# Latent attention by heads: q's mean and root, the place of k, values of two pairs at once, and the output by tiles

## What is computed

```python
cq, ckv, k_rope = split(h @ w_dqkv, [384, 640])              # latents: 384, 256, 32
q  = (rms_norm(cq) @ w_uq).reshape(.., 16 heads, 96)         # 64 plain + 32 turned
kv = (rms_norm(ckv) @ w_ukv).reshape(.., 16 heads, 128)      # 64 of k, 64 of v
q_nope, k_nope = rms_norm(q_nope), rms_norm(k_nope)          # by head
q_rope, k_rope = apply_rope(rms_norm(q_rope)), apply_rope(rms_norm(k_rope))
s = (q_nope . k_nope + q_rope . k_rope) * 96 ** -0.5         # causal
o = softmax(s) @ v;   x = x + o @ w_o
```

## Time and profile before

| | us |
|---|---|
| median of three runs | 2913.57 |
| the runs | 2916.39, 2913.57, 2913.35 |
| the profiled execution, its own time | 2916.41 |
| its span | 2914.6 |
| PE busy in the span | 2871.7 |
| DVE, ACT, POOL busy | 1300.5, 567.2, 1849.9 |
| mean granted clock of PE, share of full speed | 0.994 |

### The profile page before, as it was taken

How to read it: one execution, slowest core, us unless ns; L and a number is a source line. 1 busy time by engine, 2 the same in 40 slices (tenths; PEclk the granted TensorE clock), 3 DMA queues, 4 the chain that set the end, 5 groups by cost and what they waited for, 6 DMA issues and landing times.

```text
span 2914.6 us, 36291 instructions
## 1 busy us (share of the span) xinstructions
PE 2871.7 (99%) x13536; PEld 2327.8 (80%) x13536; DVE 1300.5 (45%) x1506; ACT 567.2 (19%) x822; POOL 1849.9 (63%) x1822
## 2 busy tenths in 40 slices
PE   9999999999989999999999999999999999999998
PEld 6778887888867778888888888788888777788887
DVE  5765544414456655414444223443244555443241
ACT  4550221000124441000111101210001445300000
POOL 5557548777752228777785565677777444577775
PEclk9999999999999999999999999999999999999999
DMA  4112212232220002222232222222322111222322
GB/s 147 64 58 87 74 57 101 88 107 101 79 89 28 33 34 87 92 103 100 80 124 82 78 94 80 73 101 79 113 85 91 69 65 50 72 88 87 106 92 88
DMA packets 38582, 242.34 MB, mean 83 GB/s; under 512 B 4288, under 2 KB 4672, under 8 KB 16608
## 3 DMA queue, kind: packets, MB, share of 16 engines
q1 hardware_dynamic: 37296, 237.19, 23.4%
q10 hardware_dynamic: 1200, 3.96, 0.4%
HBM read 239.04 MB, written 2.10 MB: 83 GB/s over the span
## 4 chain that ended last, share of the span: by engine, by line
PE 92%; DVE 3%; POOL 1%; ACT 1%; DVEq 1%; issue 1%; ACTq 0%; DMA 0%; POOLq 0%; SPq 0%
PE ps L400 66%; PE ps L433 12%; PE ps L1344 1%; PE ps L1159 1%; PE ps L1300 1%; PE ps L1381 1%; POOL w_lo L702 1%; PE ps L1178 1%; PE ps L1361 1%; PE ps L1376 1%; PE ps L1394 1%; PE ps L1290 1%; POOL w_hi L714 1%; DVEq L2257 0%; DVEq L1852 0%
## 5 line engine op out<-in xcount | busy, mean ns | idle before, releaser
L714 POOL CAST w_hi<-raw 128x512 fp32r<-128x512 f32 (+1 forms) x909 | 677.4, 761 | 1047.3 <-PE ps L400 838.1
L702 POOL TENSOR_TENSOR w_lo<-raw,w_hi 128x512 fp32r<-128x512 f32 (+1 forms) x909 | 1222.0, 1356 | 0.1
L400 PE MATMUL ps<-h_hi,w_hi 128*128 128x512 f32 x1904 | 751.9, 395 | 3.3 <-DVE h_lo L1863 3.0
L400 PE MATMUL ps<-h_hi,w_lo 128*128 128x512 f32 x1904 | 742.0, 390 | 0.0
L400 PE MATMUL ps<-h_lo,w_hi 128*128 128x512 f32 x1904 | 741.5, 389 | 0.0
L400 PEld LDWEIGHTS ps<-h_hi,w_hi 128*128 128x128 f32 x1904 | 357.7, 188 | 80.7 <-issue 5.0
L400 PEld LDWEIGHTS ps<-h_lo,w_hi 128*128 128x128 f32 x1904 | 357.9, 188 | 75.8 <-issue 3.1
L400 PEld LDWEIGHTS ps<-h_hi,w_lo 128*128 128x128 f32 x1904 | 357.6, 188 | 75.2
L400 PE MATMUL ps<-a_hi,w_hi 128*128 128x512 f32 x816 | 320.1, 392 | 2.2 <-issue 1.4
L400 PE MATMUL ps<-a_lo,w_hi 128*128 128x512 f32 x816 | 318.4, 390 | 0.0
L400 PE MATMUL ps<-a_hi,w_lo 128*128 128x512 f32 x816 | 318.3, 390 | 0.0
(11 more groups left out here) (320 smaller groups left out, 3623.5 us busy)
## 6 DMA issues: line engine op xcount, KB each, us to landing
raw<-weights SPq DMA_DIRECT2D x169, 1024.0 KB, 4.9
raw<-weights SPq DMA_DIRECT2D x64, 704.0 KB, 4.1
raw<-weights SPq DMA_DIRECT2D x8, 640.0 KB, 3.9
raw<-weights SPq DMA_DIRECT2D x8, 512.0 KB, 3.6
x<-x_in SPq DMA_DIRECT2D x8, 256.0 KB, 6.9
x_out<-x SPq DMA_DIRECT2D x1, 2048.0 KB, 6.3
scr<-phase_ret ACTq DMA_DIRECT2D x1, 1536.0 KB, 8.0
scr<-phase_mla ACTq DMA_DIRECT2D x1, 640.0 KB, 6.7
```

Source lines behind the costliest of these rows:

```text
L400: mm = pe.matmul(out_ap, a, b, start=(i == 0 and not begun), stop=(i == n - 1 and ended))
L702: pool.tensor_tensor(w_lo[:, slot, parts[j]], raw[:, slot, parts[j]], w_hi[:, slot, parts[j]].bitcast(F32), ALU.subtract).then_inc(s_split ...
L714: pool.tensor_copy(w_hi[:, slot, piece], raw[:, slot, piece]).then_inc(s_hi[j], 1)
```

## The change

1. **q by heads.** The mean of q's squares of head 0 moves ahead of the turned scores of head 0 on PE. ACT takes the root of each head by itself, and DVE norms and turns each head by itself (512 columns an instruction instead of 1024).
2. **k earlier.** The product for k stands between the two turned scores. Where the pair has no v of its own to make, this product is the last reader of its chunk and gives the slot back.
3. **v of two pairs.** Even pairs' chunks hold v of two pairs (1536 columns), odd pairs' chunks none (1024). The product for v has 24 matmuls of 256 columns for two pairs, in two halves of 12, in banks 7 and 6. It is made in odd pairs, before the k mean and between the two products with the weights; for pairs 0 and 1 it is made ahead of the loop. ACT copies it out in four pieces.
4. **Head of the stage.** PE takes the first q mean when the kv root is there. DVE norms kv latent 0 before the second low part of q's squares, writes one copy of the turned k, and leaves the constants; ACT writes the constants and the second copy of the turned k.
5. **The output** is stored by eight DMAs, each when its tile of x is updated.

The diff, cut to what the prediction speaks of:

```diff
...
-STAGE_WIDTHS = {"ssd": [384] + [2048] * 15, "gla": [2048] * 15, "mla": [2048] * 3 + [1280] * 8 + [2048] * 4,
+STAGE_WIDTHS = {"ssd": [384] + [2048] * 15, "gla": [2048] * 15, "mla": [2048] * 3 + [1536, 1024] * 4 + [2048] * 4,
...
-            sp.wait_ge(s_res, 8 * n_res + 2)
-            sp.dma_start(out, x[:, :, :]).then_inc(s_out, 16)
-            sp.wait_ge(s_out, 16)
+            for k in range(KD):
+                sp.wait_ge(s_res, 8 * (n_res - 1) + k + 3)
+                sp.dma_start(out[:, k, :], x[:, k, :]).then_inc(s_out, 16)
+            sp.wait_ge(s_out, 16 * KD)
...
-                def kv_weights(par, k, at):
-                    at += 768 + 256 * k
-                    return [b[:, (c0 + 3 + par) % 2, at:at + P] for b in (w_hi, w_lo)]
+                def kv_weights(par, k, at, n):
+                    at += 768 + (P if par else 3 * P) * k
+                    return [b[:, (c0 + 3 + par) % 2, at:at + n] for b in (w_hi, w_lo)]
 
                 def proj_k(w, par):
                     pe.wait_ge(s_mln, 2 * w + 1)
-                    product(pe, ps[:, 6, :], [(*kv_weights(par, k, 0), h_hi[:, k, :], h_lo[:, k, :])
-                                              for k in range(2)]).then_inc(s_mpk, 1)
-
-                def proj_v(w, par):
-                    pe.wait_ge(s_mln, 2 * w + 2)
-                    for tb in range(TB):
+                    product(pe, ps[:, 6, :], [(*kv_weights(par, k, 0, P), h_hi[:, k, :], h_lo[:, k, :])
+                                              for k in range(2)]).then_inc(s_used if par else s_mpk, 1)
...
+                def proj_v(w, part):
+                    if part == 0:
+                        pe.wait_ge(s_mln, 2 * w + 2)
+                    else:
+                        pe.wait_ge(s_mr, 3 * w + 3)
+                    for tb in (2 * part, 2 * part + 1):
                         s = slice(tb * P, (tb + 1) * P)
-                        mm = product(pe, ps[:, 7, s], [(h_hi[:, k, s], h_lo[:, k, s], *kv_weights(par, k, P))
-                                                       for k in range(2)])
-                    mm.then_inc(s_used, 1)
...
-                def q_means(w):
-                    for e in range(2):
-                        pe.wait_ge(s_msl, 2 * w + e + 1)
-                        pe.matmul(ps[:, 6 + e, :], m_blkq, m_sqh[:, e, :], start=True, stop=False)
-                        pe.matmul(ps[:, 6 + e, :], m_blkq, m_sql[:, e, :], start=False, stop=True).then_inc(s_mm, 1)
+                        mm = product(pe, ps[:, 7 - part, (tb % 2) * 256:(tb % 2) * 256 + 256],
+                                     [(h_hi[:, k, s], h_lo[:, k, s], *kv_weights(0, k, P, 2 * P)) for k in range(2)])
+                    mm.then_inc(s_used if part else s_mvp, 1)
+
+                def q_mean(w, e):
+                    pe.wait_ge(s_msl, 2 * w + e + 1)
+                    pe.matmul(ps[:, 6 + e, :], m_blkq, m_sqh[:, e, :], start=True, stop=False)
+                    pe.matmul(ps[:, 6 + e, :], m_blkq, m_sql[:, e, :], start=False, stop=True).then_inc(s_mm, 1)
...
@@ -1206,19 +1211,24 @@
                         residual_begun("mla", (0, 1))
                     max_turned(u, 0)
                     max_turned(u, 1)
-                    if not ahead:
+                    if ahead:
+                        q_mean(u + 1, 0)
+                    else:
                         residual_begun("mla", (2,))
                     scores_turned(u, par, 0)
                     if ahead:
-                        q_means(u + 1)
+                        q_mean(u + 1, 1)
+                        proj_k(u + 1, nxt)
                     else:
                         residual_begun("mla", (3,))
                     scores_turned(u, par, 1)
                     if ahead:
-                        proj_k(u + 1, nxt)
-                        proj_v(u + 1, nxt)
+                        if par:
+                            proj_v(u + 1, 0)
                         k_mean(u + 1)
                     weighted(u, par, 0)
+                    if ahead and par:
+                        proj_v(u + 1, 1)
                     weighted(u, par, 1)
...
                 proj_q(0, 0, 0)
                 latent_sum(0, (3, 4))
                 proj_q(0, 0, 1)
-                q_means(0)
+                pe.wait_ge(s_mcr, 3)
+                q_mean(0, 0)
+                q_mean(0, 1)
                 pe.wait_ge(s_mh, 5)
                 proj_k(0, 0)
                 k_mean(0)
                 proj_v(0, 0)
+                proj_v(0, 1)
+                pe.wait_ge(s_mkrope, 2)
                 pair(0, 0, True, True)
...
+                act.activation(m_ident, phase_const("mla", "mla_ident"), ACT.Copy)
+                act.activation(m_mask, phase_const("mla", "mla_mask"), ACT.Copy)
+                act.activation(m_blkq, const("blkq"), ACT.Copy)
+                for e in range(2):
+                    act.activation(h_hi[:, 6 + e, :], x[:, e, :], ACT.Copy, scale=0.0)
...
-                def q_rstd(w):
-                    for e in range(2):
-                        act.wait_ge(s_mm, 3 * w + e + 1)
-                        act.activation(m_r[:, e, :], ps[:, 6 + e, :], ACT.Ln, bias=EPS).then_inc(s_mln, 1)
-                    settled().activation(m_r[:, 0:2, :], m_r[:, 0:2, :], ACT.Exp, scale=-0.5).then_inc(s_mr, 1)
-
-                def k_squared(w):
-                    act.wait_ge(s_mpk, w + 1)
+                def q_rstd(w, e):
+                    act.wait_ge(s_mm, 3 * w + e + 1)
+                    act.activation(m_r[:, e, :], ps[:, 6 + e, :], ACT.Ln, bias=EPS).then_inc(s_mln, 1)
+                    settled().activation(m_r[:, e, :], m_r[:, e, :], ACT.Exp, scale=-0.5).then_inc(s_mr, 1)
+
+                def k_squared(w, odd, n):
+                    if odd:
+                        wait_used(c0 + 3 + w)
+                    else:
+                        act.wait_ge(s_mpk, n + 1)
...
-                def pair(u, par, first, ahead):
+                def pair(u, par, ahead, n):
                     if ahead:
                         q_squared(u + 1)
+                        q_rstd(u + 1, 0)
                     exps(u, 0)
                     if ahead:
-                        q_rstd(u + 1)
+                        q_rstd(u + 1, 1)
+                        k_squared(u + 1, not par, n)
                     exps(u, 1)
                     if ahead:
-                        k_squared(u + 1)
-                        v_copied(u + 1, 1 - par, first)
                         k_rstd(u + 1)
+                    if ahead and par:
+                        v_copied(u + 1, n, 0, 0)
                     sums_inverted(u, 0)
+                    if ahead and par:
+                        v_copied(u + 1, n, 0, 1)
                     sums_inverted(u, 1)
-
+                    if ahead and par:
+                        for part in range(2):
+                            v_copied(u + 2, n, 1, part)
+
+                q_squared(0, True, (0,))
                 latent_rstd(3, m_csq[3], 0)
-                q_squared(0, True)
-                q_rstd(0)
-                k_squared(0)
+                q_squared(0, True, (1,))
+                q_rstd(0, 0)
+                q_rstd(0, 1)
+                k_squared(0, False, 0)
                 k_rstd(0)
-                v_copied(0, 0, True)
-                pair(0, 0, True, True)
+                act.wait_ge(s_mkrope, 1)
+                act.activation(m_k[64:112, 1, :, :], m_k[64:112, 0, :, :], ACT.Copy).then_inc(s_mkrope, 1)
+                for slot in range(2):
+                    for part in range(2):
+                        v_copied(0, 0, slot, part)
+                pair(0, 0, True, None)
...
                     dve.tensor_tensor(m_k[64:112, w, :, :], over_heads(m_kx[64:112, :]), over_heads(m_t[64:112, 0, :]),
-                                      ALU.add)
-
-                for w in range(2):
-                    rope_in_k(w)
+                                      ALU.add).then_inc(s_mkrope, 1)
+
+                rope_in_k(0)
...
-                def q_normed(w):
+                def q_ready(w, par, e):
                     dve.drain()
-                    dve.wait_ge(s_mr, 2 * w + 1)
...
+                    dve.wait_ge(s_mr, 3 * w + e + 1)
+                    dve.scalar_tensor_tensor(m_raw[:, e, :], m_raw[:, e, :], m_qgain, m_r[:, e, :], ALU.mult, ALU.mult)
                     dve.drain()
-                    turned_products(m_t, m_raw[:, 0:2, :], True)
-
-                def q_ready(par):
-                    dve.tensor_tensor(m_q[:, par, :, :], m_raw[:, 0:2, :], over_heads(cos), ALU.mult)
-                    settled().tensor_tensor(m_q[64:112, par, :, :], m_q[64:112, par, :, :], m_t[64:112, :, :], ALU.add)
+                    turned_products(m_t[:, e, :], m_raw[:, e, :])
+                    dve.tensor_tensor(m_q[:, par, e, :], m_raw[:, e, :], cos, ALU.mult)
```

(21 more changed lines are left out.)

44 lines of the change are left out of this document (24 added, 20 removed).

## The result

The changed kernel takes 2900.22 us (median of 4, 2898.72 to 2901.02), the kernel before in the same session 2914.82 (median of 4, 2913.35 to 2916.39): a ratio of 0.995, 95% interval 0.9938 to 0.9962. It is 14.6 us faster. The prediction was 2894 with a range of 2887 to 2900: the sign was right, the gain was forecast a third too large, and the time lies just above the range. The two profiled executions stand at 2916.41 and 2900.19 us, 16.2 apart where the sum said 20.0.

A forecast was written before the change was run, and what follows sets the result against it. TensorE (PE), busy 99% of the span, was taken as the bound. Terms -3.6 - 7.1 - 2.6 - 2.4 + 2.8 - 7.1 = -20.0 us gave 2893.6 on the median of 2913.57, stated as 2894, range 2887 to 2900.

The forecast's parts named there:

- DVE's new wait: Loop, scores after pairs 0, 2, 4, 6: PE waits 0.7 us for DVE's k each time, +2.8 us (0 to 8.4).
- S + 21.4: Even pairs: k ready 21.4 us after S, the start of a pair's scores, before POOL's cost of 2.3 us.
- S + 23.0: Even pairs: PE reaches the next scores 23.0 us after S, the start of a pair's scores.
- a rival of 3%: Scores after pairs 0, 2, 4, 6: waits grow to 3 us and the clock falls, +27 us, 2921; 3%.
- q's order by heads: Turned scores, seven pairs: head 0's mean fills PE's wait of about 0.34 us for DVE, -2.4 us.
- V of two pairs: Loop, pairs 2 to 7: 24 matmuls of 256 columns take 2.88 us for two pairs, not 5.26; -7.1 us.
- the -2.6 in pair 0: First pair's body: loses its whole V, since pair 1's V is made ahead of the loop; -2.6 us.
- The head: Start of the latent attention stage: -7.1 us, 5.2 from the earlier start and 1.9 from the scores' clock.
- Store by tiles: Kernel's end: seven of eight 256 KB stores land under PE's matmuls, the last takes 2.7 us; -3.6 us (-1.8 to -4).
- The fit that the prediction quotes for it: Output store: about 2.0 us plus bytes at 436 GB/s, 2.6 us for 256 KB, making the term -3.7.
- the clock comes back late: Stage's head: clock back only at 881.9, scores mostly at 1.2 GHz, -4.3 instead of -7.1, 2896 us; 22%.
- POOL blocks DVE outright: Even pairs: POOL's 4.2 us wholly in DVE's way, wait 2.1 in pairs 0, 2, 4, 6, +5.6, 2899 us; 15%.

## Why the prediction was wrong, step by step

- **The step that failed: DVE's new wait, +2.8 us forecast, 7.7 measured, and 1.7 more of clock.** Its mechanism was the right one, and its price too: POOL beside DVE was put at 2.3 us and measured at 2.35. Three inputs were off. k without POOL was ready at S + 21.55, 21.95, 21.70 and 21.70, not S + 21.4 (1.3 us over the four pairs). PE arrived at S + 22.73, not S + 23.0 (the terms written there give 23.08), since the steps by heads saved more than the shown wait (0.3, four times, 1.1). And "both casts and both subtractions of the 1024-wide chunk" was taken for all four even pairs, though behind pair 6 comes the output product's chunk of 2048 columns: 3.51 us instead of some 1.4, 2.1 more, and then the clock. 2.8 + 1.3 + 1.1 + 2.1 = 7.3, near the 7.7. The order of the chunks was in the code, and nothing of pair 6 had to be guessed.
- **The clock after a wait.** The forecast had it as a rival of 3% that needs 3 us in all even pairs. It came in one pair, at 3.5 us. With q's roots together it came in all four, at 4.3 each; its total of +27 us was met there by parts that were each off, which is luck.
- **q's order by heads: -2.4 forecast.** B of the kernels without V of two pairs gives -5.0 in six pairs, so about -5.8 in seven. The waits view shows 0.34 us per pair. In the pair of the earlier trace rows another 0.07 us of idle time lies ahead of the scores, which that view does not list, and with q by heads both are 0. The remaining 0.4 lies in the distances of starts, 0.1 of it right behind the wait at the scores; the rest is not placed. This error ran against the first.
- **V of two pairs: -7.1 in the loop**, measured -7.3; the -2.6 in pair 0 was not measured by itself. Costed exactly, since 256-column matmuls stood elsewhere in the trace.
- **The head: -7.1**, measured -7.9 in the two profiles (889.29 to 881.43), of which 0.5 arose before the stage. But its parts were other than told: the new order gives 4.0 and V's width 3.4. And against the second profile of the kernel before the whole of A falls by 5.6 to 6.0, not 9.0 to 9.4. The forecast took one execution's long low stretch as the kernel's own; on the medians that part is worth less.
- **The rest.** Store by tiles -3.6, measured -4.2 in the traces and -4.4 in the medians: the last tile landed after 2.0 us, not 2.7. The fit that the prediction quotes for it stands in the Trainium skill (DMA: Bandwidth & Descriptors, Anatomy of one DMA) for DMAs that GpSimd issues, and this store is issued by SP. The rival "the clock comes back late" did not happen. "POOL blocks DVE outright" gave 2899, next to the result, by luck: POOL took 2.3 to 2.35 us of DVE's time in pairs 0, 2 and 4 and not 4.2, and the 4.5 in pair 6 come from twice the chunk. The Trainium skill (SBUF — State Buffer, SBUF: two separate sides) speaks of an exclusive lock for a whole instruction. The rows show both engines' instructions longer, DVE's step 1.66 us against 0.69 alone and POOL's subtraction 1.7 against 1.27. In pair 2 DVE lost 2.35 us and POOL 1.2 (5.0 instead of 3.8), so the full price does not fall on DVE. Whether the two take turns by whole instructions within these rows, no run here tells.
- **The sum.** Profile against profile: head -7.9, loop with its waits -7.2, clock at pair 7 +1.7, the fall near 2500 us +1.4, store -4.2: -16.2. The error of 3.8 us there is 2.1 in the loop (the waits' 4.9, less the 2.8 by which the rest of the loop fell further than forecast), 1.7 of the clock and 1.4 near 2500 us, less 0.8 in the head and 0.6 at the store. Between the medians it is 5.4. The range ended at 2900 because its upper rival priced the wait at 5.6 us over the forecast with nothing for a fall of the clock after it.

## What to carry to other kernels

When a change moves the point at which a buffer is given back, list for every iteration what the next owner does with it, the last iterations too, and which engine works beside it; a signal can be given later than it could be, and here that was worth 10 us for one moved increment. Price a new wait together with the clock that it may cost. Before making PE faster, or keeping its clock up, look for who makes its next input: in this stage's head a full clock brought 0.7 us, and the wait that followed took more. And when two profiles are compared, list the stretches at the low clock in both over the whole program, also where nothing was changed.

## What the runs showed of the hardware

- Before a pair's scores a wait of 1.1 to 1.6 us of PE left the granted clock at 1.00 in all four profiles that have such waits; at waits of 2.49, 3.5 and 3.8 to 4.4 us it went to 0.50, 1.6 to 2.9 us lost each time. I had not expected the 2.49. The length of the wait does not settle it: at the wait of 2.2 us for POOL near 455 us the clock falls in twelve of the fourteen profiles and not in the other two.
- In the head, after PE had stood repeatedly, the clock came back 2.9 to 4.0 us after V of 256 columns began, in all eight profiles that have it there at the low clock. With V of 128 columns it took 9.3 to 10.8 us in four of five profiles, PE being busy without a gap (872.80 to 883.00 above), and 2.5 us in the second profile of the kernel before. Why, no run here tells.
- The same program's low stretch in the head was 20.5 us in one profile and 13.7 in another, and another program had 10.2 us at the low clock before 460 us in one profile and none in the other. A single profile's stretch at the low clock is no constant of the kernel.
- DVE pays for POOL as POOL does for DVE: DVE's last steps of q and k took 2.35 us more beside two casts and two subtractions, which take 2 x 0.61 + 2 x 1.27 = 3.8 us where DVE is idle (882.75 and 883.88 in the profile before) and took 5.0 beside DVE.
- A store of 256 KB landed 2.0 us after its issue when it went out by itself, under PE's work or not (the last three); five that were issued within 2.3 us landed after 5.3 to 5.8 us each.
